# The expert stretch of a hybrid decoder layer on one core: larger weight transfers, and output sums that stay in PSUM

## The chip, the core and the metric

The kernel runs on one core of a Trainium2 chip. The core has TensorE (matmuls, from SBUF into the eight PSUM banks), VectorE and ScalarE (elementwise work), GpSimd (POOL) and SyncE (SP), whose instruction queue issues most of the DMA transfers here. The engines run side by side and wait for each other by semaphores. The metric is the device time of one execution in microseconds (us); less is better.

## The reference, cut to what matters

One layer over 16 learned and 256 given tokens of width 1024, all in float32. A mixing sub-layer comes first (sliding-window attention beside a state-space mixer, gated, summed, projected by `w_out`); the change leaves it alone but for a few loads. Then comes a top-4-of-32 expert network on the 256 tokens:

```
logits = u @ w_router + b_router;  top_w = softmax(top 4 of logits)
for each expert e, for the tokens tok routed to it with weights wt:
    hh = u[tok] @ w1[e] + b1[e]                 # 1024 -> 2048
    h  = min(hh[0::2],7) * sigmoid(1.702*min(hh[0::2],7)) * (clip(hh[1::2],-7,7) + 1)
    out[tok] += (h @ w2[e] + b2[e]) * wt        # 1024 -> 1024
out = rms_norm(residual + out) * g_final
```

The weights of one expert are 8 MiB (w1) and 4 MiB (w2); all 32 are read, 402.7 MB in all.

## The kernel before, in words

Everything before the expert stretch is a fixed program that ends with `w_out`, the norm and the router at about 560 us. In its last part TensorE multiplies by `w_out` for the first 128 tokens (c = 0) and then for the second (c = 1); between the chunks of c = 1 it transposes the normalised rows of c = 0 and computes their logits. VectorE adds the residual (L1036), scales the rows to `un` (L1043), and splits `un` into three bfloat16 parts `upart` (L1044 to L1048), which together hold the float32 value. Then it finds the four experts of each token and each token's place among its expert's rows (L1062 to L1087).

The expert stretch is a loop over 32 experts, the same in every engine's program, two experts per turn of TensorE's and SP's loops (even and odd). CAP = 64 rows are computed per expert; were an expert to get more tokens, further passes would run (`more`), which does not happen with these inputs. For expert t:

- VectorE makes one-hot matrices from the places (`gsel`, `gwt`, `bsel`; L1091 to L1094, function `routing`).
- TensorE gathers the tokens by 48 small bfloat16 matmuls with `gsel`, and starts the hidden sum in PSUM by the bias rows `b1all` (4 matmuls). VectorE copies the gathered rows, times the norm's gain, to `usel` (L1107).
- TensorE multiplies by w1 in eight parts of 1 MiB, first the four of hidden columns 0 to 1023 (half 0), then those of half 1. Each part is 4 matmuls of 512 columns with 64 stationary columns; two such matmuls fill the two halves of a PSUM bank's partitions.
- Between the halves it scatters the output of expert t-1: four matmuls of the weighted one-hot `s2` with `ysb`, each into bank 6 or 7, and VectorE adds each result to `acc` in SBUF (L1103), before the bank is used again. Then it transposes `gwt` (L1527), and ScalarE copies that to `s2` (L755).
- VectorE and ScalarE compute the clamped SwiGLU of each half (L1115 to L1119, L758). TensorE transposes the hidden rows (L1535), ScalarE copies them to `hT` (L761), and TensorE multiplies by w2 in four parts of 1 MiB. Half 1 is transposed after the w2 parts of half 0. The result lies in banks 2 and 3; ScalarE copies both to `ysb` (L765).

The weights arrive by SP's queue in parts of 128 partitions x 2 x 1024 numbers, so in runs of 4 KiB. Twelve of the parts go to the twelve slots of `ring`. Parts 0 to 3 have a second buffer for odd experts, in `arena` (`DOUBLED`), so 16 MiB can be under way or waiting. `step` sets the order of SP's queue: parts 0 to 3 of the next expert as this one's predecessor frees them, then parts 4 to 11 of this one; before each SP waits for `slot_used`, which TensorE raises after each part. `first_experts` and two places in the list of earlier chunks issue the first 16 parts as the mixing sub-layer frees the memory. After the loop come the last scatter, the sum of squares (L777), the reciprocal root on POOL (L494), the final scaling (L1160) and the store (L481).

All matmuls are issued by one helper, so they stand under L1169. A float32 matmul is two instructions in the profile.

## Time and profile before

| | us |
|---|---|
| median of 3 runs (1538.6 to 1541.98) | 1541.2 |
| the profiled execution: span from first to last instruction | 1541.4 |
| TensorE busy | 1397.1 (91%) |
| VectorE busy | 503.4 (33%) |
| ScalarE busy | 321.0 (21%) |
| first gather of the expert stretch begins | 559.8 |
| last w2 matmul ends | 1527.8 |

The profiled execution's own time is the span; it agrees with the median of the other runs to 0.2 us. The chip is asked for 470.77 MB in all, 305 GB/s over the span. The page divides the span into 40 slices of 38.5 us and shows for each the busy share of an engine in tenths, the granted TensorE clock in tenths of 2.4 GHz, and DMA. A busy engine need not be the one that decides; what decides in a stretch is read from who waits for whom there.

### The profile page before, as it was taken

The numbers are of one execution on the slowest core, as the hardware profiler recorded it, in microseconds if no ns is written. First come the engines' busy times: TensorE is split into PE (matmuls) and PEld (weight loads), VectorE is DVE, ScalarE is ACT, GpSimd is POOL, SyncE is SP. The second block draws the span as 40 slices with busy tenths as digits, with TensorE's granted clock in tenths as the row PEclk, the third lists the DMA queues.
The fourth block names the chain that finished last, engine by engine and source line by source line (L and its number), as shares of the span: only waits on it lengthen the run. The fifth ranks groups of instructions, "written<-read, shape, count | busy, mean of one in ns | idle before, by whom it ended". The sixth has DMA issues, their size and how long they took to land.

```text
span 1541.4 us, 19865 instructions
## 1 busy us (share of the span) xinstructions
PE 1397.1 (91%) x7262; PEld 679.1 (44%) x7262; DVE 503.4 (33%) x1075; ACT 321.0 (21%) x642; POOL 23.3 (2%) x33
## 2 busy tenths in 40 slices
PE   6359999999999969999999999999999999999997
PEld 3238878755588533333333333333333333333332
DVE  1004546657723253223223322322332232223223
ACT  3002433334410021211121121112112111211121
POOL 2010000000000000000000000000000000000000
PEclk9769999999999979999999999999999999999999
DMA  9996144314293579999999999999999999999993
GB/s 180 104 220 215 55 126 145 113 55 109 69 293 136 198 245 401 410 410 409 409 410 410 410 410 409 409 410 410 410 410 410 409 409 410 410 410 410 409 409 131
DMA packets 165814, 470.77 MB, mean 305 GB/s; under 512 B 24198, under 2 KB 59246, under 8 KB 165748
## 3 DMA queue, kind: packets, MB, share of 16 engines
q1 hardware_dynamic: 162544, 457.27, 78.3%
q0 software_dynamic: 2880, 12.63, 5.2%
q10 hardware_dynamic: 356, 0.41, 0.1%
q8 instruction: 21, 0.34, 0.1%
q14 instruction: 13, 0.11, 0.0%
HBM read 462.42 MB, written 7.60 MB: 305 GB/s over the span
## 4 chain that ended last, share of the span: by engine, by line
PE 72%; SPq 12%; DMA 8%; DVE 4%; ACT 2%; issue 1%; ACTq 0%; POOL 0%; POOLq 0%; DVEq 0%
PE bank L1169 70%; SPq L401 7%; DMA ring<-in_w 6%; SPq L414 5%; DVE arena L1107 1%; DMA ring<-in_w_in 1%; ACT arena L761 1%; DVE arena L1115 1%; ACT arena L758 1%; PE bank L1535 1%; DMA rows<-in_g_ssm 0%; PE bank L1527 0%; PE bank L1254 0%; PE bank L1429 0%; PE bank L1256 0%
## 5 line engine op out<-in xcount | busy, mean ns | idle before, releaser
L1169 PE MATMUL bank<-ring,arena 128*64 128x512 f32 (+3 forms) x2808 | 677.1, 594 | 53.9 <-ACT arena L761 45.6
L1169 PEld LDWEIGHTS bank<-ring,arena 128*64 128x64 f32 (+2 forms) x2808 | 219.2, 141 | 435.5 <-issue 365.6
L1169 PE MATMUL bank<-arena 128*128 128x64 bf16 (+6 forms) x2773 | 370.9, 337 | 13.8 <-DVE arena L1073 4.1
L1169 PE MATMUL bank<-arena,ring 128*128 128x256 f32 (+1 forms) x1184 | 276.4, 392 | 46.5 <-DMA ring<-in_w_in 43.9
L1169 PEld LDWEIGHTS bank<-arena 128*128 128x128 bf16 (+3 forms) x2773 | 173.4, 125 | 221.0 <-issue 145.9
L1169 PEld LDWEIGHTS bank<-arena,ring 128*128 128x128 f32 x1184 | 227.8, 195 | 85.3 <-issue 45.7
L1103 DVE TENSOR_TENSOR arena<-arena,bank 128x512 f32<-128x512 f32 x128 | 87.9, 687 | 292.4 <-PE bank L1169 292.4
L1107 DVE TENSOR_TENSOR arena<-bank,cols 128x512 f32<-128x512 f32 x32 | 22.1, 691 | 292.5 <-PE bank L1169 292.5
L755 ACT ACTIVATE arena<-bank 128x256 f32<-128x256 f32 x32 | 12.3, 383 | 360.1 <-PE bank L1527 360.1
L758 ACT ACTIVATE arena<-arena 128x256 f32<-128x256 f32 x64 | 26.6, 416 | 172.3 <-DVE arena L1115 172.3
L765 ACT ACTIVATE arena<-bank 128x512 f32<-128x512 f32 x64 | 34.7, 595 | 127.0 <-PE bank L1169 127.0
L1115 DVE TENSOR_SCALAR arena<-bank 128x256 f32<-128x256 f32 x64 | 27.1, 424 | 80.5 <-PE bank L1169 75.7
L761 ACT ACTIVATE arena<-bank 128x256 f32<-128x256 f32 x64 | 24.0, 374 | 132.9 <-PE bank L1535 132.9
L755 ACT ACT_TABLE_LOAD x32 | 41.1, 1283 | 0.6
L758 ACT ACT_TABLE_LOAD x32 | 41.1, 1283 | 0.6
L1535 PEld LDWEIGHTS bank<-squares,arena 128*128 128x128 f32 x128 | 12.9, 141 | 51.9 <-issue 51.9
L818 DVE TENSOR_TENSOR dts<-dts,dtb 128x96 f32<-128x96 f32 x1 | 0.3, 259 | 89.8 <-ACT dts L594 89.8
L1535 PE MATMUL bank<-squares,arena 128*128 128x128 f32 x128 | 28.0, 301 | 0.0
L1119 DVE TENSOR_TENSOR arena<-arena 128x256 f32<-128x256 f32 x64 | 27.2, 425 | 2.2
L1117 DVE SCALAR_TENSOR_TENSOR arena<-arena 128x256 f32<-128x256 f32 x64 | 27.2, 425 | 2.2
L1116 DVE TENSOR_SCALAR arena<-bank 128x256 f32<-128x256 f32 x64 | 27.1, 424 | 2.2
L494 POOL TENSOR_TENSOR rstd<-ssq,half_neg 128x1 f32<-128x1 f32 (+2 forms) x7 | 6.2, 888 | 1347.4 <-DVE ssq L1158 974.9
(221 smaller groups left out, 593.3 us busy)
## 6 DMA issues: line engine op xcount, KB each, us to landing
ring<-in_w SPq DMA_DIRECT2D x320, 1024.0 KB, 18.3
arena<-in_w SPq DMA_DIRECT2D x64, 1024.0 KB, 18.2
ring<-in_w_in SPq DMA_DIRECT2D x30, 1024.0 KB, 5.5
ring<-in_w_ssm SPq DMA_DIRECT2D x8, 1024.0 KB, 5.9
toep_rows<-arena POOLq DMA_DIRECT2D x1, 6400.0 KB, 68.6
ring<-in_w_in SPq DMA_DIRECT2D x16, 256.0 KB, 9.2
ring<-in_w_att SPq DMA_DIRECT2D x16, 256.0 KB, 6.5
ring<-in_w_out SPq DMA_DIRECT2D x4, 1024.0 KB, 4.8
```

The lines of the kernel that those rows point to most:

```text
L401: sp.dma_start(dst, src).then_inc(loaded, 16)
L414: sp.dma_start(dst(n % FSLOTS), src).then_inc(slot_loaded[n % FSLOTS], 16)
L755: sc.activation(s2, bank[5][:, 0:SEQ], ACT.Copy).then_inc(s2_saved, 1)
L758: sc.activation(sig[:, half, :], glu[:, half, :], ACT.Sigmoid, scale=ALPHA).then_inc(esig_ready, 1)
L761: sc.activation(hT[:, half, :, :], bank[5][:, 0:256].rearrange("p (b n) -> p b n", b=2), ACT.Copy).then_inc(hT_saved, 1)
L765: sc.activation(ysb[:, n, :], bank[2 + n][:, :], ACT.Copy).then_inc(ye_saved, 1)
L1103: done(v.tensor_tensor(a, a, bank[6 + n][:, :], ALU.add), sc_added, s * 4 + (i + 2))
L1107: done(v.tensor_tensor(usel, bank[4][:, :].rearrange("p (k s) -> p k s", k=KT), col_gffn.unsqueeze(2).to_broadcast([P, KT, CAP]), ALU.mult ...
L1115: done(v.tensor_scalar(glu[:, half, :], hv[:, :, 0], LIMIT, None, ALU.min), glu_ready, t * 2 + half + 1)
L1117: ch.link(v.scalar_tensor_tensor(lin[:, half, :], lin[:, half, :], 1.0, glu[:, half, :], ALU.add, ALU.mult))
L1169: return tn.matmul(o, lhsT, rhs, start=first, stop=last, skip_group_check=True)
L1535: ins = tn.transpose(bank[5][:, P * q:P * q + P], hsw[:, half, P * q:P * q + P], ident)
```

## The change

- w1's parts are rows 2p and 2p+1 of a block of 256 rows for partition p, all 2048 columns: 16 KiB in one run. A part is 2 MiB, and there are four. w2's two parts of 2 MiB hold two rows of 1024 next to each other, twice: runs of 8 KiB. The order of the contraction rows changes with it, so `un`, the norm's gain, the router's weights and the transposes of `hsw` take their elements with a stride.
- Six parts have a buffer for even experts, the four of w1 a second one for odd experts: ten buffers, 20 MiB. The first loads are spread anew over the waits of the earlier program.
- The output sum lies in banks 0 to 3 over all experts. It starts with the residual, put there by identity matmuls (`residual`), and the scatter adds to it in place. VectorE's additions go. w2's result is one bank: output columns 0 to 511 on partitions 0 to 63, the rest on partitions 64 to 127. The scatter's four matmuls contract over 64 rows each, the upper or the lower half.
- TensorE's order within an expert: bias rows, all of w1, the gather for expert t+1, the scatter of t-1, the transposes of the slot weights, all four transposes of hidden rows, w2. `usel` of t+1 is thus made during expert t.
- The final sum of squares and scaling read PSUM.

```diff
+        even_bufs = [at(6400, BUF), ring_pair(4), at(R, BUF), at(R + 6144, BUF), ring_pair(1), ring_pair(5)]
+        odd_bufs = [ring_pair(0), ring_pair(2), ring_pair(3), at(0, BUF)]
+        DOUBLED = range(len(odd_bufs))
...
+        w1_v = w1.rearrange("e (s p k) c -> e s p (k c)", p=P, k=2)
+        w2_v = w2.rearrange("e (h c p q) n -> e h p c (q n)", p=P, c=2, q=2)
...
+            src = [w1_v[ahead:][one, s].rearrange("e p f -> p (e f)") for s in range(4)]
+            src += [w2_v[ahead:][one, h].rearrange("e p c f -> p (e c) f") for h in range(2)]
...
+                    for i in range(2):
                         fetch(i, sources[0][i], 0)
-                    fetch(DOUBLED[2], sources[1][DOUBLED[2]], 1)
+                if n == co[0]:
+                    sp.wait_ge(tile_ready, T_END)
+                    fetch(2, sources[0][2], 0)
...
             def first_experts():
...
+                sp.wait_ge(branch_used, 12)
+                fetch(3, sources[0][3], 0)
+                fetch(4, sources[0][4], 0)
+                sp.wait_ge(m_done, 8)
+                fetch(5, sources[0][5], 0)
+                sp.wait_ge(h_ready, 2)
+                for i in range(3):
                     fetch(i, sources[1][i], 1)
-                for i in range(SLOTS):
-                    if slot_of(i) in late:
-                        sp.wait_ge(h_ready, 2)
-                        fetch(i, sources[0][i], 0)
-                sp.wait_ge(topexp_in, 1)
-                fetch(DOUBLED[3], sources[1][DOUBLED[3]], 1)
+                sp.wait_ge(lg_ready, 1)
+                fetch(3, sources[1][3], 1)
...
+                    pool.wait_ge(up_done, 1)
...
-                    pool.dma_start(gfin, bass.AP(g_fin.tensor, 0, [[0, P], [1, D]])).then_inc(gfin_in, 16)
+                    pool.wait_ge(b2_cleared, 1)
+                    for half in range(2):
+                        pool.dma_start(ysb[CAP * half:CAP * half + E, :], b2[:, 512 * half:512 * half + 512]).then_inc(b2_in, 16)
...
+            def s2_save(n):
+                act.wait_ge(s2_ready, n + 1)
+                sc.activation(s2, bank[6][:, 0:SEQ], ACT.Copy).then_inc(s2_saved, 1)
...
+                s2_save(t + 1)
...
-                act.wait_ge(slot_used, t * 12 + 12)
-                for n in range(2):
-                    sc.activation(ysb[:, n, :], bank[2 + n][:, :], ACT.Copy).then_inc(ye_saved, 1)
+                act.wait_ge(slot_used, t * PARTS + PARTS)
+                sc.activation(ysb, bank[6][:, :], ACT.Copy).then_inc(ye_saved, 1)
...
-            for c in range(2):
-                act.wait_ge(acc_final, 2 * c + 2)
-                squared(sc.activation(at(0, D), acc[:, c, :], ACT.Square,
-                                      accum_out=ssq[:, c:c + 1]), 13 + c + 1)
+            for i in range(4):
+                act.wait_ge(last_sc_ready, i + 1)
+                squared(sc.activation(glu.rearrange("p a b -> p (a b)"), bank[i][:, :], ACT.Square,
+                                      accum_out=ssq[:, i:i + 1]), 13 + i + 1)
...
+                dve.wait_ge(resid_done, c + 1)
                 ch.link(v.tensor_tensor(ures[:, c, :], un[:, c, :], upart[:, 0, c, :], ALU.subtract))
...
-                ch.link(v.tensor_copy(upart[:, 2, c, :], ures[:, c, :]))
+                done(v.tensor_copy(upart[:, 2, c, :], ures[:, c, :]), up_done, c + 1)
...
+            def slots_of(col):
                 for c in range(2):
...
-            def scatter_add(s):
-                for i in range(4):
-                    c, n = divmod(i, 2)
-                    dve.wait_ge(sc_ready, s * 4 + (i + 1))
-                    a = acc[:, c, 512 * n:512 * n + 512]
-                    done(v.tensor_tensor(a, a, bank[6 + n][:, :], ALU.add), sc_added, s * 4 + (i + 2))
+                    ins = v.tensor_scalar(gsel[:, c, :], iota2[:, 0:CAP], pos[:, c, bass.ds(col, 1)], None, ALU.is_equal)
+                ins.then_inc(g_ready, 1)
...
+            def slot_weights(col, n):
+                dve.wait_ge(s2_ready, n)
+                for c in range(2):
+                    ins = v.tensor_scalar(gwt[:, c, :], iota2, pos[:, c, bass.ds(col, 1)], wtok[:, c, bass.ds(col, 1)],
+                                          ALU.is_equal, ALU.mult)
+                ins.then_inc(gw_ready, 1)
+            def usel_save(n):
+                dve.wait_ge(gat_ready, n + 1)
+                v.tensor_tensor(usel, bank[7][:, :].rearrange("p (k s) -> p k s", k=KT),
+                                col_gffn.unsqueeze(2).to_broadcast([P, KT, CAP]), ALU.mult).then_inc(usel_ready, 1)
...
+                    if half == 0:
+                        dve.wait_ge(hid_ready, t + 1)
+                    else:
+                        dve.wait_ge(slot_used, t * PARTS + 4)
+                    hv = bank[4 + half][:, :].rearrange("p (f two) -> p f two", two=2)
...
+                usel_save(t + b + 1)
+                slots_of(e + 2)
+                bias_row(e + 1)
+                slot_weights(e + 1, t + 2)
...
-            for i in range(4):
-                c, n = divmod(i, 2)
-                dve.wait_ge(last_sc_ready, i + 1)
-                a = acc[:, c, 512 * n:512 * n + 512]
-                done(v.tensor_tensor(a, a, bank[6 + n][:, :], ALU.add), acc_final, i + 1)
...
+                for n in range(2):
+                    ins = v.scalar_tensor_tensor(fin[:, c, 512 * n:512 * n + 512], bank[2 * c + n][:, :], rstd[:, 4 + c:5 + c],
+                                                 gfin[:, 512 * n:512 * n + 512], ALU.mult, ALU.mult)
...
+            def residual(c):
+                pe.wait_ge(h_done, 2 * c + 2)
+                for n in range(2):
+                    ins = mm(bank[2 * c + n][:, :], ident, acc[:, c, 512 * n:512 * n + 512], True, True)
+                ins.then_inc(resid_done, 1)
...
+                        residual(0)
...
+            residual(1)
...
-            def scatter(s):
-                for i in range(4):
-                    c, n = divmod(i, 2)
-                    if i < 2:
-                        pe.wait_ge(sc_added, s * 4 + 1)
-                    else:
-                        pe.wait_ge(sc_added, s * 4 + i)
-                    mm(bank[6 + n][:, :], s2[:, P * c:P * c + P], ysb[:, n, :], True, True).then_inc(sc_ready, 1)
...
+            def gather(n):
+                pe.wait_ge(g_ready, n + 1)
...
+            def scatter(n):
+                pe.wait_ge(ye_saved, n + 1)
+                pe.wait_ge(s2_saved, n + 1)
+                for c in range(2):
+                    for half in range(2):
+                        r = slice(CAP * half, CAP * half + CAP)
+                        ins = mm(bank[2 * c + half][:, :], s2[r, P * c:P * c + P], ysb[r, :], False, True)
...
+                pe.wait_ge(usel_ready, t + b + 1)
+                for i in range(4):
...
-                    if half == 0:
-                        pe.wait_ge(ye_saved, t * 2 + 2)
-                        scatter(t)
-                        for c in range(2):
-                            ins = tn.transpose(bank[5][:, P * c:P * c + P], gwt[:, c, :], ident)
-                        ins.then_inc(s2_ready, 1)
-                pe.wait_ge(s2_saved, t + 1)
+                                c0 = 1024 * half + 512 * c
+                                ins = mm(bank[4 + half][64 * c:64 * c + 64, :], usel[:, k, :], w[:, kk, c0:c0 + 512],
+                                         False, k == KT - 1)
+                        if i == 3 and half == 0:
+                            ins.then_inc(hid_ready, 1)
...
+                gather_wait = t * 1 + b * 2 + 1
+                gather(gather_wait)
+                scatter(t)
+                weight_transposes(t + b + 1)
                 for half in range(2):
                     pe.wait_ge(hs_ready, t * 2 + half + 1)
-                    if half:
-                        pe.wait_ge(hT_saved, t * 2 + 1)
                     for q in range(2):
-                        ins = tn.transpose(bank[5][:, P * q:P * q + P], hsw[:, half, P * q:P * q + P], ident)
+                        ins = tn.transpose(bank[4 + half][:, P * q:P * q + P], hsw[:, half, q::2], ident)
                     ins.then_inc(hT_ready, 1)
+                pe.wait_ge(s2_saved, t + 2)
+                for half in range(2):
...
+                    expert_arrived(pe, 4 + half, t, pair, odd)
+                    w = expert_buf(4 + half, odd)[0].rearrange("p (c q n) -> p c q n", c=2, q=2)
...
+                            for n in range(2):
+                                ins = mm(bank[6][64 * n:64 * n + 64, :], hT[:, half, q, 64 * c:64 * c + 64],
+                                         w[:, c, q, 512 * n:512 * n + 512],
+                                         half == 0 and c == 0 and q == 0, half == 1 and c == 1 and q == 1)
...
+            gather(0)
+            weight_transposes(0)
+            pe.wait_ge(b2_in, 32)
             pe.wait_ge(b1_spread, 32)
+            pe.wait_ge(flag_ready, 1)
```

What stands on three queues before and now. First TensorE, from the last w1 part of half 0 of an odd expert to the start of w2. Before (`sc_added` is raised by VectorE's additions, `more_loaded` and `slot_loaded` by weight transfers):

```order
L1169 MATMUL bank<-arena 64x512 [waits more_loaded3]
L1169 MATMUL bank<-arena 64x512 x3
L1524 ISA
L1492 ISA [waits ye_saved]
L1169 MATMUL bank<-arena 128x512 [waits sc_added] x2
L1494 REGISTER_ALU
L1169 MATMUL bank<-arena 128x512 [waits sc_added]
L1494 REGISTER_ALU
L1169 MATMUL bank<-arena 128x512 [waits sc_added]
L1527 MATMUL bank<-squares,arena 128x128 x2
L374 ISA
L1169 MATMUL bank<-ring,arena 64x512 [waits slot_loaded11]
```

And now, from the last w1 part of an odd expert on:

```order
L1194 MATMUL bank<-arena 64x512 [waits odd_loaded3]
L1194 MATMUL bank<-arena 64x512 x7
L1522 REGISTER_ALU
L1194 MATMUL bank<-arena 128x64 [waits g_ready]
L1194 MATMUL bank<-arena 128x64 x47
L1194 MATMUL bank<-arena 128x512 [waits s2_saved,ye_saved]
L1194 MATMUL bank<-arena 128x512 x3
L1534 MATMUL bank<-squares,arena 128x128 [waits gw_ready]
L1534 MATMUL bank<-squares,arena 128x128
L1572 ISA
L1574 MATMUL bank<-squares,arena 128x128 [waits hs_ready]
L1574 MATMUL bank<-squares,arena 128x128
```

The gather and the scatter have moved between w1 and the transposes of the hidden rows, and the waits for VectorE's additions between the scatter's matmuls are gone.

Second TensorE at the end of `w_out`, before the first expert. Before, the last `w_out` chunk follows the router's matmuls, and the transposes of c = 1 follow that:

```order
L1169 MATMUL bank<-wrt,arena 128x32 [waits u2_saved]
L1169 MATMUL bank<-wrt,arena 128x32 x3
L1169 MATMUL bank<-ring,arena 128x512 [waits slot_loaded0]
L1169 MATMUL bank<-ring,arena 128x512 x3
L1444 MATMUL bank<-squares,arena 128x128 [waits un_ready]
L1444 MATMUL bank<-squares,arena 128x128 x7
```

Now:

```order
L1194 MATMUL bank<-wrt,arena 128x32 [waits u2_saved]
L1194 MATMUL bank<-wrt,arena 128x32 x3
L1194 MATMUL bank<-arena,squares 128x512 [waits h_done]
L1194 MATMUL bank<-arena,squares 128x512
L1194 MATMUL bank<-ring,arena 128x512 [waits slot_loaded0]
L1194 MATMUL bank<-ring,arena 128x512 x3
L1194 MATMUL bank<-arena,squares 128x512 [waits h_done]
L1194 MATMUL bank<-arena,squares 128x512
L1472 MATMUL bank<-squares,arena 128x128 [waits un_ready]
```

Two pairs of identity matmuls have come in, one ahead of the last chunk and one behind it.

SP's queue keeps the order of its parts, w1 of the next expert and then the rest of this one; the transfers per expert fall from twelve to six. The last two experts are issued as before: the single parts of expert 30, then all of expert 31.

## Rows read from the trace of the kernel before

**Rows 1.** The page's 40 slices: DMA share in tenths, rate.
```profile
DMA  9996144314293579999999999999999999999993
GB/s 180 104 220 215 55 126 145 113 55 109 69 293 136 198 245 401 410 410 409 409 410 410 410 410 409 409 410 410 410 410 410 409 409 410 410 410 410 409 409 131
```

**Rows 2.** DMA issues to the ring: number, size, median us to landing.
```profile
ring<-in_w SPq DMA_DIRECT2D x320, 1024.0 KB, 18.3
```

**Rows 3.** Timeline, VectorE's usel operation: start, duration, idle before.
```profile
1254.29 0.69 DVE L1107 TENSOR_TENSOR arena<-bank,cols 128x512 f32<-128x512 f32 x1 [9.84 <-PE bank L1169]
1285.01 0.69 DVE L1107 TENSOR_TENSOR arena<-bank,cols 128x512 f32<-128x512 f32 x1 [9.92 <-PE bank L1169]
```

**Rows 4.** Weight queue's waits for DMA, 600 to 1200 and 1225 to 1500.
```profile
PEld bank L1169 <- DMA ring<-in_w: 0.3, 1, 0.3
...
PEld bank L1169 <- DMA ring<-in_w: 27.3, 32, 1.2
```

**Rows 5.** Timeline of TensorE over one expert.
```profile
995.20 7.09 PE L1169 MATMUL bank<-ring,arena 128*64 128x512 f32 x32
1002.22 0.44 PE L1535 MATMUL bank<-squares,arena 128*128 128x128 f32 x2
1003.53 3.65 PE L1169 MATMUL bank<-ring,arena 128*64 128x512 f32 x16 [0.88 <-ACT arena L761]
1007.12 0.44 PE L1535 MATMUL bank<-squares,arena 128*128 128x128 f32 x2
1008.11 3.65 PE L1169 MATMUL bank<-ring,arena 128*64 128x512 f32 x16 [0.55 <-ACT arena L761]
1011.69 2.13 PE L1169 MATMUL bank<-arena 128*128 128x64 bf16 x52
1014.05 10.98 PE L1169 MATMUL bank<-arena 128*64 128x512 f32 x40 [0.23 <-DVE arena L1107]
1024.86 0.38 PE L1527 MATMUL bank<-squares,arena 128*128 128x128 f32 x2
1025.17 7.09 PE L1169 MATMUL bank<-ring,arena 128*64 128x512 f32 x32
```

**Rows 6.** Windows: stretch, length, five engines, granted clock, DMA share, GB/s.
```profile
380.00:390.00 10.00, 10.00 (x38) 5.48 (x37) 6.54 (x11) 3.41 (x6) 0.00 (x0) 1.00 0.26 83
464.00:467.00 3.00, 3.00 (x15) 2.66 (x14) 0.00 (x0) 0.00 (x0) 0.00 (x0) 1.00 0.95 331
516.00:530.00 14.00, 14.00 (x34) 6.25 (x33) 3.00 (x6) 1.15 (x2) 0.83 (x2) 1.00 1.00 352
1400.00:1500.00 100.00, 93.24 (x562) 32.99 (x558) 25.31 (x55) 19.06 (x31) 0.00 (x0) 1.00 1.03 410
1510.00:1515.00 5.00, 5.00 (x23) 1.91 (x24) 3.51 (x9) 1.99 (x3) 0.00 (x0) 1.00 0.50 202
```

**Rows 7.** Timeline of SP's queue: late first loads, the first freed part.
```profile
541.15 2.23 SPq L401 DMA_DIRECT2D ring<-in_w  x4
...
566.04 26.07 SPq L401 DMA_DIRECT2D ring<-in_w  x12
```

**Rows 8.** Timeline ahead of the first expert, VectorE and TensorE.
```profile
531.97 1.23 DVE L1047 TENSOR_TENSOR arena<-arena 128x1024 f32<-128x1024 f32 x1
533.23 0.69 DVE L1048 CAST arena<-arena 128x1024 bf16<-128x1024 f32 x1
...
537.44 3.68 PE L1169 MATMUL bank<-ring,arena 128*128 128x512 f32 x8
541.23 1.42 DVE L1036 TENSOR_TENSOR arena<-bank,arena 128x512 f32<-128x512 f32 x2 [7.31 <-PE bank L1169]
563.28 7.69 PE L1169 MATMUL bank<-ring,arena 128*64 128x512 f32 x32
```

**Rows 9.** Timeline of the last w2 matmuls and the store.
```profile
1524.16 3.65 PE L1169 MATMUL bank<-ring,arena 128*64 128x512 f32 x16 [0.55 <-ACT arena L761]
1529.16 3.93 PE L1169 MATMUL bank<-arena 128*128 128x512 f32 x8 [1.35 <-ACT arena L765]
```

More of the change, by code:

```diff
@@ L55 @@
 FSLOTS = 7
+PARTS = 6
+BUF = 2 * SLOT
 NEG = -1e30
@@ new lines, in hybrid_layer @@
+        ysb = at(4224, 512)
+        rt = at(4736, 16, 64)
+        glu, sig = at(4736, 2, 256), at(5248, 2, 256)
+        s2 = at(5760, SEQ)
+        gwt = at(6016, 2, P)
+        usel = at(R + 4096, KT, CAP)
+        hT = at(R + 4608, 2, 2, P)
+        lin = hsw = at(R + 5120, 2, 256)
+        SM = R + 13312
+        gsel = at(SM, 2, CAP, dt=BF16)
+        bsel = at(SM + 64, CAP, dt=BF16)
+        pos = at(SM + 96, 2, 40)
+        wtok = at(SM + 176, 2, 40)
+        ident3 = at(SM + 256, 40)
@@ L399, in fetch @@
             def fetch(i, src, odd):
-                dst, loaded = expert_slot(i, odd)
+                dst, loaded = expert_buf(i, odd)
+                if i >= 4:
+                    dst = dst.rearrange("p (c f) -> p c f", c=2)
                 sp.dma_start(dst, src).then_inc(loaded, 16)
@@ L442, in single @@
             def single(sources, odd, used):
-                for i in range(DOUBLED.stop, SLOTS):
+                for i in range(DOUBLED.stop, PARTS):
                     sp.wait_ge(slot_used, used + (i + 1))
@@ L1174, in _ @@
             tn.transpose(bank[4][:, 0:120], rows[0:120, 0, :], ident[0:120, 0:120])
-            tn.transpose(bank[4][:, 128:160], rows[0:32, 1, :], ident[0:32, 0:32]).then_inc(rows_T, 1)
+            tn.transpose(bank[4][:, 128:152], rows[0:24, 1, :], ident[0:24, 0:24])
+            for k in range(2):
+                ins = tn.transpose(bank[4][:, 160 + 4 * k:164 + 4 * k], gffn4[0:4, k::2], ident[0:4, 0:4])
+            ins.then_inc(rows_T, 1)
             pe.wait_ge(tab_ready, 1)
@@ L1508, in expert @@
                         c0 = 1024 * half + 512 * c
-                        mm(bank[half][64 * c:64 * c + 64, :], bsel[0:3 * E, :], b1all[0:3 * E, c0:c0 + 512], True, False)
-                pe.wait_ge(usel_ready, t + 1)
-                for half in range(2):
-                    for s_ in range(4):
-                        i = 4 * half + s_
-                        expert_arrived(pe, i, t, pair, odd)
-                        w, _ = expert_slot(i, odd)
+                        mm(bank[4 + half][64 * c:64 * c + 64, :], bsel[0:3 * E, :], b1all[0:3 * E, c0:c0 + 512], True, False)
@@ L1555, in _ @@
                 with pe.Fori(0, PASSES - 1) as b:
+                    gather(b * G_PASS + G_PASS)
                     with pe.Fori(0, E // 2) as pair:
```

273 lines of the change are left out of this document (117 added, 156 removed).

## The prediction

> **What bounds the kernel now.** I read the page's slices first [rows 1]: from slice 17 to 39 the DMA row stands at 9 and the GB/s row at 409 to 410. TensorE is busy there too, 93.24 of 100 us in the window from 1400 us [rows 6]. So for some 900 of 1541.4 us two resources are full at once, and the busy shares can't say which one sets the pace. The DMA issues [rows 2] say what the traffic is: transfers of 1 MiB, twelve per expert, of which ten go to the ring. Each lands 18 us after its issue, so seven are under way at a time and DMA never lacks work. Next the distance between experts: on TensorE 29.97 us from the second half of w1 to the next [rows 5], later, by VectorE's one usel operation per expert, 30.72 (1254.29 to 1285.01 [rows 3]). The weight queue's waits separate the two [rows 4]: between 600 and 1200 us TensorE waited for a weight transfer once (0.3 us), between 1225 and 1500 us 32 times (27.3 us). 12 MiB (12.58 MB) in 30.72 us is 409.6 GB/s, exactly the saturated rate. So the first 20-odd experts run at TensorE's own period of 30.0 us, eating up what had been loaded ahead, and the last nine or so at the transfers' 30.7. A change of this stretch has to shorten both, or it gives at most 0.7 us on a third of the experts.
>
> TensorE's 29.97 us of one expert [rows 5], start to start: first half of w1 with the scatter 10.81 (1014.05 to 1024.86), of which the half itself is 7.02 (995.20 to 1002.22, the other half alone), so the scatter 3.79; transposes of the slot weights 0.31 (to 1025.17); second half of w1 7.02; transposes of the hidden rows and the wait for ScalarE's copy 1.31; w2 3.59; the same wait again 0.99; w2 3.58; gather, bias rows and the wait for usel 2.36.
>
> **What the change does to TensorE's period.** The weight matmuls stay: 32 and 16 of them, 14.04 and 7.17 us. Gather and bias rows stay, 2.13 us (52 instructions), but their 0.23 us wait for usel goes, since gather n+1 now runs behind w1 of expert n and usel is ready 10 us early. Slot-weight transposes 0.31. The hidden rows' four transposes are issued together, so one of the two waits for ScalarE remains: 1.31 instead of 1.31 + 0.99. VectorE has time: half 0 is released four matmuls (1.8 us) before w1 ends, its chain of four 0.42 us operations and that of half 1 end 2.1 us behind w1, and TensorE is then still in gather and scatter (1.6 + 1.7 us). The scatter has four matmuls of 512 columns as before, without the VectorE additions between them. The trace does not show a matmul with 64 contraction rows beside another one, so I bound it: at the dearest it costs what the row of eight instructions says without waits, some 3.5 us; at the cheapest the two 64-row halves run side by side, as the two 64-column halves of the weight matmuls do (two of them every 0.88 us, 7.02 / 8, against 0.87 to 0.95 for one full-width matmul), 1.75 us. I take the cheap end, the likeness to the column halves being close; both are kept.
> Period: 14.04 + 7.17 + 2.13 + 0.31 + 1.31 + 1.75 = 26.7 us; with the dear scatter 28.5.
> The Trainium skill (TensorEngine Tiling (Array Packing), section Tiling Modes) lists two 64x128 tiles that run in parallel, which gives the 1.75 us, but adds that a change of tiling mode drains the engine; by that the scatter could be some tenths dearer, and no row here shows a drain's price.
>
> **What it does to the transfers.** Four w1 transfers with 16 KiB runs and two w2 transfers with 8 KiB runs take the place of twelve with 4 KiB runs; the bytes are the same. The windows [rows 6] give the price of a run from share and rate. 4 KiB runs: 410 GB/s at share 1.03, so 4096 x 16 x 1.03 / 410 = 164.6 ns a packet. 1 KiB runs (the w_ssm chunks): 1024 x 16 x 0.95 / 331 = 47.0 ns in one window, 51.3 in another (0.26, 83). A straight line through them rises by (164.6 - 47.0) / 3 = 39.2 ns per KiB and leaves 7.8 ns per packet, or by (164.6 - 51.3) / 3 = 37.8 and leaves 13.5. Carried on to 16 KiB that is 635 or 618 ns, so 16384 x 16 x 1.03 / 635 = 425 GB/s, or 437; to 8 KiB 321 or 316 ns, so 420 or 428. I take values nearer to the low line, whose window has the fuller DMA: 428 and 422. The ends of the unknown, since no queue of SP shows runs over 4 KiB: no gain (410), above 437, and below the worst 4 KiB stretch, 352 GB/s at share 1.00.
> The Trainium skill (DMA: Bandwidth & Descriptors, section Where 436 GB/s comes from) puts the ports' ceiling at 435 GB/s. By that my upper line is cut by 2 GB/s, and the gain can't pass 6%; the trace, at 410, is under the ceiling.
>
> A transfer period is then 8.39 MB / 428 + 4.19 MB / 422 = 19.60 + 9.94 = 29.5 us, above TensorE's 26.7 and 28.5. So the transfers become the bound early, and stay it.
>
> **Before the first expert.** Before, the last of the 16 MiB of first loads were four parts when h was ready, at 541.15, and one behind the logits; then none until the first part was used, at 566.0 [rows 7]. Now 4 MiB go out when y is done, as before, 2 ahead of w_out (SP waits there for the last transposes of the branch stage, behind which w_out's loads are queued; they are done by then), 6 at the end of the branch products, 6 when h is ready and 2 at the logits: 20 MiB. What is added to the path there: the residual sum enters PSUM by two 512-column identity matmuls ahead of the last w_out chunk, at 0.92 us each (3.68 / 4 [rows 8]), +1.8 us on everything behind. VectorE's splitting of u for the first 128 tokens now waits for that, until about 539.3 (537.44 + 1.8), and takes 4.0 us with its gaps (1.23 + 0.69 twice), to 543.3; behind it stands the h addition that began at 541.23. So +2.1 in all, not +1.8. The second pair of identity matmuls lies in the time in which TensorE waits for the norm of c = 1. The normalised rows are written with a stride; for that I put 0.4. Against that, the gather of expert 0 waits for two selection operations rather than five: three fewer, -1.1. Behind VectorE's wait for the residual nothing else queues but those operations, and POOL's queue (the clearing of ysb, two b2 transfers, then the next rstd) is through at about 545, before the sum of squares is, which begins with that h addition's end. w1 of expert 0 starts at 563.28 + 2.1 + 0.4 - 1.1 = 564.7, and its first 2 MiB are free after half of 7.69 us: 568.5.
>
> **The sum.** In the run before, 16 of 384 MiB were issued before 566.0; the other 368 MiB are 385.9 MB, 941.2 us at 410; the stream ended at 1512.5 (window 1510 to 1515: share 0.50), 946.5 us after 566.0, so 5.3 us went with getting up to speed. I keep these. After: 364 MiB remain at 568.5. SP issues w2 of expert 30 before w1 of expert 31, and from the landing of expert 29's w2 on, 16 MiB are left (39 us of transfers) but two whole experts of TensorE (53 us), so TensorE bounds the end. Until that landing: 232 MiB of w1, 243.3 MB / 428 = 568.4 us, and 116 MiB of w2, 121.6 MB / 422 = 288.2. Landing at 568.5 + 5.3 + 568.4 + 288.2 = 1430.4. Then the last half of w2 3.6 and two experts, 53.4: 1487.4. The cross-check by TensorE alone, 564.7 + 32 x 26.7 = 1419 (1477 with 28.5), lies below, so the transfers decide. The end: before, 13.6 us from w2's last matmul (1527.8) to 1541.4 [rows 9]. One PSUM copy less -0.5, the scatter 3.93 to about 2.0 and no VectorE additions -2.2; four half-size squares on ScalarE with their sums instead of two +0.9: 11.8. Total 1487.4 + 11.8 = 1499 us. The profiled span of before is 1541.4, the median of the runs 1541.2, so nothing is to be converted. 2.7% faster. Where it comes from: transfers' rate some 34 us, deeper preloading and the shorter period of TensorE the rest.
>
> **The rivals.**
> A. Longer runs are no faster: the fixed part lies per 4 KiB, not per run. For it: no SP transfer here has a longer run. Against: packets of 1 and 4 KiB lie on a line with a fixed part. 364.9 MB / 410 = 890.0, landing at 1463.8, + 57.0 + 11.8 = 1532.6. Chance 0.14.
> B. TensorE stays the bound: scatter unpaired and a wait of 1.5 us more (for s2 or the hidden rows, which no longer have a w1 half between them): period 30, 564.7 + 960 + 11.8 = 1536.5. Against: every releaser has slack of 1 us or more in the working above. Unpaired alone costs only 2 x 1.8 at the end: 1503. Chance 0.04.
> C. Slower than before: the long runs lower the rate, as they would if reading rows 16 KiB apart in step, or filling one partition for 0.6 us on end, cost the memories something. Decisive is 406 GB/s: (1541.4 - 11.8 - 57.0 - 5.3 - 568.5) = 898.8 us for 364.9 MB. At 400 GB/s the landing is at 1486.1 and the time 1555; at the 352 of [rows 6] it is 1679. For it: the 352 itself, 4 KiB runs that did not reach 410 when they began with other traffic. Against: 900 us at 410 with w1's rows 8 KiB apart. Chance 0.07.
> [...]
> D. The upper line, 437 and 428: 556.7 + 284.2 us, so 1483.5. It is part of the forecast's own range.
>
> **How the numbers follow.** Forecast case 0.73, from 1484 to 1512; A 0.14, B 0.04, C 0.07, and 0.02 for a step I don't see. Range: from 1484 up to A's and B's place with their uncertainty, 1536; outside lie C and the remains. What a measurement can tell from no change is 0.2%, 3 us: under 1538.1 lie the forecast, A in most of its spread and half of B: 0.87; within 0.2%: 0.05; above: 0.08.
>
> **What would show it.** A GB/s row of about 425 in slices 16 to 37 and larger transfers; distances between usel operations of 26 to 27 us for the first experts (28.5: scatter unpaired) and 29.5 later; TensorE's waits for DMA at the w2 parts, some 2.8 us per expert; the scatter's eight instructions in under 2 us; usel of expert 0 some 1.4 us later; the end in 12 us. Wrong it would be with 410 in that row (A), less (C), or waits on ScalarE or VectorE in the place of DMA (B).

## The result, and the profile after

| kernel | median of the runs | range | profiled span |
|---|---|---|---|
| before | 1541.59 us | 1538.6 to 1542.06 | 1541.4 us |
| changed | 1497.48 us | 1495.86 to 1497.97 | 1496.1 us |

The ratio is 0.9715, with a 95% interval of 0.9703 to 0.9728: 44.1 us or 2.85% faster. Forecast were 1499 us, within 1484 to 1536.

The page's slices of the changed kernel, which answer to [rows 1]: DMA share in tenths, then the rate.

```profile
DMA  9997134322367458999999999999999999999994
GB/s 183 104 203 251 58 107 140 119 85 57 113 232 239 173 226 365 427 427 425 426 428 427 423 427 428 427 424 427 427 426 425 429 427 424 427 428 427 424 379 177
```

The DMA row is as full as it was, so a share of 9 says nothing of whether more would go through. The rate says it: 427 where it was 410. The page's list of DMA issues (number, size, median us from issue to landing) shows what makes the stream now; before, it was one row of 1 MiB transfers [rows 2].

```profile
ring<-in_w SPq DMA_DIRECT2D x128, 2048.0 KB, 25.6
arena<-in_w SPq DMA_DIRECT2D x64, 2048.0 KB, 29.5
```

The chain that ended last, shares of the span by engine. Before, it held 72% TensorE and 8% DMA; now DMA holds 43%.

```profile
PE 47%; DMA 43%; SPq 5%; DVE 2%; ACT 1%; issue 1%; ACTq 0%; POOL 0%; DVEq 0%; POOLq 0%
```

An early expert on the timeline of TensorE, which answers to [rows 5] (start, duration, group; in brackets the idle time before it and what ended it):

```profile
661.54 7.09 PE L1194 MATMUL bank<-ring,arena 128*64 128x512 f32 x32 [0.46 <-ACT arena L764]
668.45 4.04 PE L1194 MATMUL bank<-arena 96*64 96x512 bf16 x20
672.32 3.61 PE L1194 MATMUL bank<-ring,arena 128*64 128x512 f32 x16
675.75 10.47 PE L1194 MATMUL bank<-arena 128*64 128x512 f32 x88
686.15 0.44 PE L1534 MATMUL bank<-squares,arena 128*128 128x128 f32 x2
686.42 0.64 PE L1574 MATMUL bank<-squares,arena 128*128 128x128 f32 x4
687.52 7.22 PE L1194 MATMUL bank<-ring,arena 128*64 128x512 f32 x32 [0.46 <-ACT arena L764]
```

From one w2 to the next it is 25.98 us (687.52 less 661.54), w2 itself 6.91 in one piece, and the only wait left is 0.46 us for ScalarE. The same engine at a late expert:

```profile
1273.54 0.64 PE L1574 MATMUL bank<-squares,arena 128*128 128x128 f32 x4
1276.46 3.65 PE L1194 MATMUL bank<-ring,arena 128*64 128x512 f32 x16 [2.29 <-DMA ring<-in_w]
1281.53 3.65 PE L1194 MATMUL bank<-ring,arena 128*64 128x512 f32 x16 [1.41 <-DMA ring<-in_w]
...
1302.98 0.64 PE L1574 MATMUL bank<-squares,arena 128*128 128x128 f32 x4
1305.98 3.65 PE L1194 MATMUL bank<-ring,arena 128*64 128x512 f32 x16 [2.36 <-DMA ring<-in_w]
```

In these two experts TensorE stands still twice, 3.7 us in all, each time ahead of a half of w2, and the distance is 29.52 (1305.98 less 1276.46). 12.58 MB in 29.5 us is 427 GB/s: the transfers set the pace. By VectorE's usel operation the 2nd to the 6th distance are 25.98 to 26.12, the 7th to the 31st 29.4 to 29.6, and the last is 25.98.

The end, TensorE's last three groups, and the end of expert 29's w2 ahead of them:

```profile
1424.03 8.78 PE L1194 MATMUL bank<-ring,arena 128*64 128x512 f32 x32 [2.36 <-DMA ring<-in_w]
1432.64 4.04 PE L1194 MATMUL bank<-arena 96*64 96x512 bf16 x20
...
1477.69 7.09 PE L1194 MATMUL bank<-ring,arena 128*64 128x512 f32 x32 [0.46 <-ACT arena L764]
1485.47 1.99 PE L1194 MATMUL bank<-arena 64*128 64x512 f32 x8 [0.69 <-ACT arena L767]
```

The scatter's eight instructions take 1.99 us, where [rows 9] had 3.93.

Expert 29's w2 has no second wait, but takes 8.78 us in one piece: the granted clock is at its lower level (1.2 GHz) from 1424.8 to 1428.2, right behind the wait of 2.36 us. A window inside that stretch (five engines, granted clock, DMA share, GB/s; the stream runs empty in it, because SP holds w2 of expert 30 back until expert 29's is used):

```profile
1426.00:1428.00 2.00, 2.00 (x8) 0.64 (x6) 0.00 (x0) 0.00 (x0) 0.00 (x0) 0.50 0.44 184
```

By the trace, 25 experts in a row, up to this one, have such a wait of 2.3 to 2.4 us ahead of w2. 10 of them have the second wait of 1.4 us as well; in the other 15 the clock falls during or just behind the first wait, and the second wait is missing. That costs nothing that shows, since the second part of w2 lands only then (at 1428.9 for expert 29). gather2, below, has no such fall of the clock and the same late distance of 29.5 us.

### The profile page after: what moved, and what is told of

Read it like the earlier page. It is cut to its first block, busy times and chain, and to the rows that moved or that the text cites. A ratio compares the mean times of both kernels' runs of the same rounds, so it can differ in the third digit from the quotient of the medians.

```text
span 1496.1 us, 18512 instructions
## 1 busy us (share of the span) xinstructions
PE 1333.6 (89%) x7320; PEld 697.8 (47%) x7320; DVE 397.9 (27%) x952; ACT 261.8 (18%) x584; POOL 22.4 (1%) x32
## 4 chain that ended last, share of the span: by engine, by line
PE 47%; DMA 43%; SPq 5%; DVE 2%; ACT 1%; issue 1%; ACTq 0%; POOL 0%; DVEq 0%; POOLq 0%
PE bank L1194 45%; DMA ring<-in_w 41%; SPq L421 5%; DMA ring<-in_w_in 1%; DMA rows<-in_g_ssm 0%; PE bank L1282 0%; PE bank L1457 0%; PE bank L1284 0%; PE bank L1534 0%; ACT arena L755 0%; DVE arena L1055 0%; DVE arena L1053 0%; PE bank L1348 0%; ACT arena L611 0%; DVE ring L908 0%
## 5 line engine op out<-in xcount | busy, mean ns | idle before, releaser
L1194 PE MATMUL bank<-ring,arena 128*64 128x512 f32 (+3 forms) x2296 | 579.0, 613 | 76.9 <-DMA ring<-in_w 72.6
L1194 PE MATMUL bank<-arena 128*128 128x64 bf16 (+7 forms) x3333 | 418.3, 372 | 11.6 <-DVE arena L1081 5.2
L1194 PEld LDWEIGHTS bank<-ring,arena 128*64 128x64 f32 (+2 forms) x2296 | 204.8, 147 | 411.2 <-issue 341.2
L1194 PEld LDWEIGHTS bank<-arena 128*128 128x128 bf16 (+4 forms) x3333 | 204.7, 126 | 226.8 <-issue 205.3
L760 ACT ACTIVATE arena<-arena 128x256 f32<-128x256 f32 x64 | 26.7, 417 | 394.4 <-DVE arena L1126 394.4
L767 ACT ACTIVATE arena<-bank 128x512 f32<-128x512 f32 x32 | 19.1, 597 | 315.6 <-PE bank L1194 315.6
L1109 DVE TENSOR_SCALAR arena<-squares,arena 128x128 f32<-128x128 f32 x66 | 19.9, 344 | 36.0 <-PE bank L1534 36.0
L755 ACT ACTIVATE arena<-bank 128x256 f32<-128x256 f32 x32 | 12.3, 383 | 93.2 <-PE bank L1534 93.2
L908 DVE SCALAR_TENSOR_TENSOR ring<-ring,cols 128x272 f32<-128x272 f32 x48 | 24.1, 502 | 1.7
L1033 DVE TENSOR_TENSOR arena<-ring,bank 128x512 f32<-128x512 f32 x8 | 5.5, 687 | 62.6 <-PE bank L1194 62.4
L764 ACT ACTIVATE arena<-bank 128x256 f32<-128x256 f32 x64 | 21.0, 385 | 0.0
L1194 PE MATMUL bank<-arena,squares 128*128 128x512 f32 x40 | 19.0, 597 | 2.1 <-DVE arena L1041 2.1
## 6 DMA issues: line engine op xcount, KB each, us to landing
arena<-in_w SPq DMA_DIRECT2D x64, 2048.0 KB, 29.5
```

What stands on the lines that cost most here:

```text
L760: sc.activation(sig[:, half, :], glu[:, half, :], ACT.Sigmoid, scale=ALPHA).then_inc(esig_ready, 1)
L764: sc.activation(hT[:, half, :, :], bank[4 + half][:, 0:256].rearrange("p (b n) -> p b n", b=2), ACT.Copy).then_inc(hT_saved, 1)
L767: sc.activation(ysb, bank[6][:, :], ACT.Copy).then_inc(ye_saved, 1)
L908: ch.link(v.scalar_tensor_tensor(o, xp[:, k:k + NT], w(k), o, ALU.mult, ALU.add))
L1109: ins = v.tensor_scalar(gwt[:, c, :], iota2, pos[:, c, bass.ds(col, 1)], wtok[:, c, bass.ds(col, 1)], ALU.is_equal, ALU.mult)
L1194: return tn.matmul(o, lhsT, rhs, start=first, stop=last, skip_group_check=True)
```

## The experiments

Every kernel below is the changed one with one edit, timed beside the kernel before on the same chip (1540.6 to 1541.2 us there; differences to the changed kernel's 1497.48 are thus good to about 1 us). In the diffs "-" is the changed kernel.

**runs4k: the changed kernel with the runs of before.** It asks whether run length is what pays.

```diff
-        w1_v = w1.rearrange("e (s p k) c -> e s p (k c)", p=P, k=2)
+        w1_v = w1.rearrange("e (s p k) (h c) -> e s p h k c", p=P, k=2, h=2)
-        w2_v = w2.rearrange("e (h c p q) n -> e h p c (q n)", p=P, c=2, q=2)
+        w2_v = w2.rearrange("e (h c p q) n -> e h p q c n", p=P, c=2, q=2)
...
-                sp.dma_start(dst, src).then_inc(loaded, 16)
+                for h in range(2):
+                    sp.dma_start(dst[:, h], src[h]).then_inc(loaded, 16)
```

> The changed kernel (1497.5 us) with each 2 MiB part loaded as two transfers of 1 MiB in runs of 4 KiB, as before; buffers, TensorE's order and PSUM sums stay as changed. Theory 1 (the run length sets the transfers' rate, and that rate sets the pace from the seventh expert on): GB/s row at 410 again, usel operations 30.7 us apart later, 26.0 at the start; some 33 us more, 1531. Theory 2 (TensorE's shorter period brought the gain, the runs little): within 5 us of 1497. If 1531 comes, the rest of the change is worth 10 us against the kernel before.

Measured: 1533.64 us (1533.24 to 1537.0), ratio to before 0.9957 [0.9943, 0.9971]. Its slices, and TensorE at a late expert:

```profile
GB/s 181 104 218 222 56 125 141 120 55 110 80 284 192 172 277 407 409 409 409 410 410 409 410 410 410 410 409 410 410 410 409 410 410 410 409 409 410 410 333 208
```

```profile
1275.19 8.87 PE L1194 MATMUL bank<-ring,arena 128*64 128x512 f32 x32 [3.42 <-DMA ring<-in_w]
...
1305.91 6.29 PE L1194 MATMUL bank<-ring,arena 128*64 128x512 f32 x20 [3.42 <-DMA ring<-in_w]
```

The rate is back at 410 and the distance at 30.72 us, with everything else of the change in place. So 36.2 of the 44.1 us are run length (1533.64 less 1497.48), and the shorter period of TensorE, the deeper stock and the shorter end together give 7 to 8. That is less than the 10 that I expected; where the rest went is open.

**runs8k: all runs 8 KiB, in 1 MiB transfers.** It parts the length of a run from the size of a transfer.

```diff
-        w1_v = w1.rearrange("e (s p k) c -> e s p (k c)", p=P, k=2)
+        w1_v = w1.rearrange("e (s p k) c -> e s p k c", p=P, k=2)
...
-                sp.dma_start(dst, src).then_inc(loaded, 16)
+                for k in range(2):
+                    sp.dma_start(dst[:, SLOT * k:SLOT * k + SLOT], src[k]).then_inc(loaded, 16)
```

> The changed kernel with each part as two transfers of 1 MiB, but all in runs of 8 KiB. Theory 1 (a fixed cost per run of 8 to 9 ns): rate 421 GB/s, periods 29.9, 1506 to 1507. If the size of a transfer (1 MiB for 2 MiB) counted and not the run, it would be as slow as with runs of 4 KiB, 1531, at 410.

Measured: 1505.05 us (1503.84 to 1507.26), 0.9771 [0.9755, 0.9787]. The window from 900 to 1000 us (five engines, granted clock, DMA share, GB/s):

```profile
900.00:1000.00 100.00, 90.67 (x540) 35.85 (x538) 14.82 (x42) 12.83 (x23) 0.00 (x0) 0.97 1.01 422
```

At 1 MiB the transfers carry 422 GB/s with 8 KiB runs and 410 with 4 KiB runs, so the gain comes without larger transfers. The reverse shows too: each run is one packet in the trace's DMA records, and an 8 KiB packet takes 314 ns on average between 900 and 1000 us, in the 1 MiB transfers here and in the 2 MiB transfers of the changed kernel alike. The run decides, not the transfer's size. The 7.6 us to the changed kernel are w1's runs, 8 KiB for 16: a late distance of 29.84 for 29.52 us.

**stock16: 4 MiB less loaded ahead.**

```diff
-                for i in range(3):
+                for i in range(2):
                     fetch(i, sources[1][i], 1)
-                sp.wait_ge(lg_ready, 1)
+                sp.wait_ge(slot_used, 1)
+                fetch(2, sources[1][2], 1)
```

> The changed kernel, but the last two of the ten first loads wait for the first freed part, so 16 MiB are loaded before the experts begin instead of 20. Theory 1: each MiB not loaded ahead comes at the end at 2.45 us, so 9.8 us more: 1507; the transfers become the bound four experts earlier. Rival (depth is without effect, the queue is full anyhow): 1497.5.

Measured: 1506.51 us (1505.03 to 1507.94), 0.9773 [0.9757, 0.9789]: 9.0 us slower than the changed kernel, where 4.19 MB at 427 GB/s are 9.8. The usel distances after the first read 25.97, 25.98, 28.32 and then 29.5. Where the transfers set the pace, what is loaded before the stretch is worth about its transfer time.

**gather2 and gather4: TensorE given more to do.** The gather's matmuls are issued twice or four times, with the same result.

```diff
-                for k in range(KT):
+                for k in [k for _ in range(4) for k in range(KT)]:
```

> The changed kernel with the 48 gather matmuls of each expert issued four times: some 4.7 us more of TensorE per expert, period 30.6 instead of 26.0. Theory 1: above the transfers' 29.5, so TensorE is the bound and only the part over it counts: 564.7 + 32 x 30.6 + 12 = 1556 to 1561, GB/s row at about 411, with the long runs unused. A theory in which TensorE's time counts in full: 1497.5 + 32 x 4.7 = 1648; one in which it doesn't count: 1497.5.

Measured for gather4: 1548.23 us (1545.72 to 1548.39), 1.0047 [1.0031, 1.0064]. The distance is 30.19 us at a late expert:

```profile
1253.77 7.09 PE L1194 MATMUL bank<-ring,arena 128*64 128x512 f32 x32 [0.46 <-ACT arena L764]
...
1283.95 7.09 PE L1194 MATMUL bank<-ring,arena 128*64 128x512 f32 x32 [0.46 <-ACT arena L764]
```

The waits for transfers are gone. A repeat costs 1.40 us, (30.19 - 25.98) / 3, less than the 1.57 that I had put (4.7 / 3), so the time came out 8 us below the range that was expected.

> The gather matmuls are issued twice, same result, one repeat costing TensorE 1.40 us per expert by the kernel with them fourfold. Theory (the transfers set the pace up to expert 29's w2, TensorE has 29.5 - 26.0 = 3.5 us of slack): distances of 27.4 at first, 29.5 later, and only the first expert's gather and the two experts behind the last landing count: 1497.5 + 1.4 + 2 x 1.4 = 1501.7, range 1499 to 1503. Rival (TensorE sets the pace for part of each period, through the waits at w2): + 32 x 1.4 = 1542; a mixture 1510 to 1520.

Measured for gather2: 1501.52 us (1500.86 to 1502.03), 0.9745 [0.9729, 0.9761], against 1501.7 forecast. The distances were 27.38 us at first and 29.5 from the tenth on. Of 32 x 1.4 = 45 us that TensorE has more to do, 4.0 show, against the 4.2 expected for the first expert's repeat and the last two experts'. The rest lies in the 3.5 us in which TensorE waits anyway.

**scatter_order and scatter_one: do the two 64-row halves run side by side?** The first only reorders the four matmuls, both of one half and then both of the other. The second sends all four to rows 0 to 63; it leaves the second half's outputs out and counts the first's twice.

```diff
 scatter_order
-                for c in range(2):
-                    for half in range(2):
+                for half in range(2):
+                    for c in range(2):
 scatter_one
-                        r = slice(CAP * half, CAP * half + CAP)
+                        r = slice(0, CAP)
```

> The changed kernel with the scatter's four matmuls in another order, both of rows 0 to 63 first, then both of rows 64 to 127. If it is the two different row halves that run side by side, only the middle two can now: the eight instructions inside an expert take some 2.6 us instead of 1.8. If each matmul is simply cheap with 64 rows, the time stays. Device time in either case within 3 us of 1497.5, since TensorE waits for transfers.

Measured, one run: 1496.81 us, and the early distances stay 25.98 to 26.00. The 2.6 us did not come. By the expectation as I had written it, this would speak for matmuls that are cheap with 64 rows, and against the halves running side by side; the next run says otherwise.

> All four scatter matmuls of an expert read rows 0 to 63 (half 0), in the loop and behind it, so the second half's outputs are left out and the first's counted twice; number and size of the matmuls stay. Theory (the two halves run side by side on the array, which is where 3.93 us became 1.99): in one half they can't, so the scatter behind the last expert takes 3.5 to 4.0 us, the distance between usel operations of the first experts is 25.98 + 1.7 = 27.7, and the time is 1497.5 + 2 x 1.7 + 0.2 = 1501. Rival (a matmul that reads 64 rows costs half of one that reads 128, alone or beside another): 1.99 us, 25.98 and 1497, as changed.

Measured, one run: 1503.08 us. The distances are 27.69, and the scatter behind the last expert:

```profile
1490.48 3.70 PE L1194 MATMUL bank<-arena 64*128 64x512 f32 x8 [0.69 <-ACT arena L767]
```

3.70 against 1.99 us, and 27.69 less 25.98 is 1.71 us, the saving forecast for the pair. So a 64-row matmul alone costs nearly what a 128-row one does (3.93 for four in [rows 9]), and it is the sharing of the array that halves it. The instruction records of an early expert show how. In the changed kernel the eight instructions start in four pairs, 7 ns apart within a pair; in scatter_one they start one by one, 0.43 to 0.54 us apart. In scatter_order they start in four pairs too, 13 ns apart, though both matmuls of the first half stand in the queue ahead of both of the second. Since two of one half don't start together, each pair must be one of each half. So the second half's work starts beside the first half's and doesn't wait for what is queued ahead of it on the other half, which is where my 2.6 us went wrong.

**endswap and allswap: w2 ahead of the next w1 in SP's queue.** In the changed kernel TensorE waits at w2 while 8 MiB of the next w1, which it needs later, go ahead of it in the queue. endswap turns the order round in the last three turns of SP's loop, allswap in every turn.

```diff
-                doubled(following, 1 - odd, used)
-                single(sources, odd, used)
+                if swap:
+                    single(sources, odd, used)
+                doubled(following, 1 - odd, used)
+                if not swap:
+                    single(sources, odd, used)
```

> The changed kernel, but for the turns of experts 27, 28 and 29 SP issues w2 of the expert ahead of w1 of the next one. Theory 1: in the transfer-bound stretch TensorE always waits for a w2 part that stands in the queue behind four w1 parts it needs later; at the end this leaves two experts (52 us) of TensorE with only 39 us of transfers beside them. With three turns swapped the last three to five experts run at 26 us: 9 to 10 us less, 1488. Rival: the queue's order doesn't matter, the same bytes are to come: 1497.5.

Measured: 1489.26 us (1487.99 to 1490.82), 0.9665 [0.9652, 0.9679]: 8.2 us faster than the changed kernel. Its last waits for transfers are these, at the third and the last of the four parts of the last w1:

```profile
1448.59 7.11 PE L1199 MATMUL bank<-ring,arena 128*64 128x512 f32 x32
1457.34 3.65 PE L1199 MATMUL bank<-ring,arena 128*64 128x512 f32 x16 [1.65 <-DMA ring<-in_w]
1462.24 7.08 PE L1199 MATMUL bank<-arena 128*64 128x512 f32 x72 [1.24 <-DMA arena<-in_w]
```

Three distances ahead of them are 25.98, where the changed kernel had one, its last. In the changed kernel 39 us of transfers follow the last one that TensorE waits for; endswap uses a part of that.

> The changed kernel with w2 of the expert ahead of w1 of the next one in every turn. Theory 1: SP's wait for the previous expert's w2 to be used then holds up w1 transfers whose buffers are long free, so that DMA stands idle in the first experts, where TensorE sets the pace, and the ten buffers are not refilled; that costs more than the end gains: some 1506, GB/s under 420 in slices 16 to 19. If only the end's balance counted: 1488.

Measured: 1503.93 us (1502.92 to 1504.52), 0.976 [0.9744, 0.9775]: 6.4 us slower than the changed kernel. Its slices tell why:

```profile
GB/s 183 104 206 245 57 112 141 114 82 73 95 259 224 199 227 156 427 426 425 428 427 425 427 428 426 424 427 427 426 424 428 427 424 427 428 427 424 427 427 248
```

The 16th slice, with the first expert in it, has 156 GB/s where the changed kernel has 365. SP's first turn now waits for w2's buffers of expert 0 (used last), and the freed w1 buffers behind that wait stay empty. From 552 to 586 us SP issues nothing, where the changed kernel's first freed part goes out at 568.8. (365 - 156) GB/s over a slice of 37.5 us is 7.8 MB, 18 us of stream in that slice; in all, the last weights land 13.6 us later than endswap's (1485.7 for 1472.2 us by the traces). The end itself is as good as endswap's, 16.9 us from that landing to the end of the span in both, but it doesn't make this good.

**both: endswap, and w2 in 16 KiB runs too.** The price of the longer runs is sixteen 64-column matmuls against the identity, where four transposes stood.

```diff
-        w2_v = w2.rearrange("e (h c p q) n -> e h p c (q n)", p=P, c=2, q=2)
+        w2_v = w2.rearrange("e (h p q) n -> e h p (q n)", p=P, h=2)
-                    for q in range(2):
-                        ins = tn.transpose(bank[4 + half][:, P * q:P * q + P], hsw[:, half, q::2], ident)
+                    for q in range(4):
+                        for c in range(2):
+                            r = slice(CAP * c, CAP * c + CAP)
+                            ins = mm(bank[4 + half][r, CAP * q:CAP * q + CAP], hsw[:, half, q::4], ident[:, r], True, True)
```

> As endswap, and w2's parts laid out so that a partition holds four successive rows: runs of 16 KiB for w2 too. The hidden rows are then transposed by sixteen matmuls with identity columns (128 x 64 x 64) instead of four transposes, at most 1 us more for TensorE, which is hidden while the transfers set the pace. Theory 1: period 29.4 instead of 29.5 and 428 GB/s throughout, 4 us under endswap less up to 3 us at the end: 1484 to 1487.

Measured: 1486.4 us (1484.23 to 1488.16), 0.9646 [0.9633, 0.966], the fastest kernel of this study, 11.1 us below the changed one. A window of it, and TensorE's timeline at the end:

```profile
900.00:1000.00 100.00, 93.91 (x629) 42.13 (x626) 15.82 (x45) 12.30 (x23) 0.00 (x0) 1.00 1.01 429
```

```profile
1437.37 2.13 PE L1197 MATMUL bank<-squares,arena 128*64 128x64 f32 x32
1439.34 7.04 PE L1197 MATMUL bank<-ring,arena 128*64 128x512 f32 x32
...
1466.24 7.04 PE L1197 MATMUL bank<-ring,arena 128*64 128x512 f32 x32
```

The rate is 429 and the late distance 29.36 us. TensorE's own period rises to 26.90 (1466.24 less 1439.34), where that is hidden. It is 2.9 us below endswap by the medians, but the two ranges touch (1487.99 to 1490.82 against 1484.23 to 1488.16), so that last step is likely rather than shown.

## Why the prediction was right, point by point

- **The bound.** Two resources were full before, and both had to become shorter. runs4k shows it from one side (TensorE at 25.98, transfers as before: 7 to 8 us), gather4 from the other (transfers as changed, TensorE slowed by added work to 30.19: 1548.23 us, 7 slower than before). Neither half of the change is worth much without the other.
- **The rate.** From rows of 1 and 4 KiB straight lines were carried on, and 422 and 428 GB/s chosen between them. Measured: 422 with 8 KiB runs alone, 429 with 16 KiB alone, 427 mixed. That there is a fixed part per run was right. That the choice met 427 so closely is luck in part: 428 at the share of 1.03 puts a 16 KiB run at 631 ns (16384 x 16 x 1.03 / 428), and it took 615 in the DMA records, at a share of 1.01. The steeper line, to which I leaned, was the wrong one (635 ns; the other gave 618), and the share that I kept at 1.03 was too high; the two nearly cancel. Rival A (the fixed part lies per 4 KiB) would have kept 410; it was priced at 1532.6 us, and runs4k, which makes 410 true, took 1533.64. Some 34 us were put to the rate, runs4k says 36.2.
- **Rival C.** No loss shows from rows 16 KiB apart or from filling a partition on end: no full slice is below 423. By the Trainium skill (DMA: Bandwidth & Descriptors, section Latency and other measured facts) copies were slower when the rows of neighbouring partitions lay 512 KiB or a larger power of two apart. In the weight loads here they lie 8 and 16 KiB apart, so no run bears this out or refutes it.
- **TensorE's period: mis-sized, 25.98 for 26.7.** w2 took 6.91 instead of 7.17 us: it runs in one piece, where I had added two of 3.59 and 3.58. Bias rows, w1, gather and scatter took 17.70 (668.45 to 686.15) instead of 14.04 + 2.13 + 1.75 = 17.92, and the transposes with their wait 1.37 (to 687.52) instead of 0.31 + 1.31. For the matmuls, durations of pieces that ended at a wait or a change of operation were a little too long for work in one piece. At the transposes the wait for ScalarE itself is shorter, 0.46 us where [rows 5] had 0.88.
- **The paired scatter.** Taking the cheap end was right: by scatter_one pairing saves 1.71 us, and 1.75 was the difference between my two ends. The term itself was a little small. From the scatter's first instruction to the first transpose behind it are 1.92 us in the instruction records, where I had put 1.75; bias rows and gather (1.94 for 2.13) and w1 (13.84 for 14.04) hid that in the sum. The Trainium skill (TensorEngine Tiling (Array Packing), section Tiling Modes) says that a change of tiling mode drains the engine. The 0.17 us would fit that, at the low end of the tenths that I had named: 0.53 us pass from the first pair to the second and from the last to the transposes, 0.43 between the others. But no run here separates a drain from other costs of beginning and ending a group.
- **Before the first expert.** The h addition began at 543.50, 2.3 us later than in [rows 8] (2.1 forecast), and the first freed part was reissued at 568.77 (568.5 forecast). That it agrees to 0.2 us is luck in part: in three kernels that are the same up to there (scatter_order, endswap, allswap) the addition begins at 542.62, 543.54 and 542.03. The two rows of the changed kernel:

```profile
543.50 1.42 DVE L1041 TENSOR_TENSOR arena<-bank,arena 128x512 f32<-128x512 f32 x2
```

```profile
568.77 0.36 SPq L406 DMA_DIRECT2D arena<-in_w  x1
```

- **The landing and the end.** Expert 29's last w2 part landed at 1428.9 (1430.4 forecast). Thence 55.9 us to the end of the last w2 at 1484.8 (57.0 forecast, with two periods of 0.7 us more), and 11.3 us to the end of the span (11.8 forecast). The sum forecast was 1499.2 for a span of 1496.1: 1.5 of the 3.1 us come from the landing, 1.1 from the last two experts, 0.5 from the end.
- **Rival B** needed a period of 30: every wait that it feared was absent but 0.46 us for ScalarE.
- **What the prediction didn't see:** that "TensorE bounds the end" was a loss one could take back. 16 MiB land unwaited-for behind the last transfer that counts; turning two groups of transfers round in three turns of the queue is worth 8 us.

## What to carry to other kernels

When two resources are full at once, price a change on each side alone: the runs with one side undone stood 8 us below the kernel before and 7 us above it, the whole change 44 below. This stream, with DMA full in both kernels, still gained 4% from longer contiguous runs, so compare GB/s, not DMA share, and read the price per packet from two run lengths that the trace has. Then look at the last awaited transfer and at what is queued ahead of it; the right order at the end of a stream need not be the right one at its start, where a wait at the queue's head leaves freed buffers empty.

## What the runs showed of the hardware

- One core's stream from memory ran at 410, 422 and 429 GB/s with runs of 4, 8 and 16 KiB. At DMA shares of 1.03, 1.01 and 1.01 that is 165, 314 and 617 ns per run on each of 16 engines (4096 x 16 x 1.03 / 410, and so on). The DMA records themselves give means of 163.7, 313.7 and 614.7 ns between 900 and 1000 us (runs4k, runs8k, both): 37.5 to 37.6 ns per KiB and a fixed 13 to 14 ns. In transfers of 1 and 2 MiB an 8 KiB run took the same 314 ns.
- Two 64-row matmuls of 512 columns on different halves of the rows share the array: 1.99 us for four, 3.70 if all use one half. Their order in the queue, alternating or both of one half first, made no difference (25.98 us early distance in both, one run of the latter).
- At 15 of the changed kernel's 25 waits of 2.3 to 2.4 us ahead of w2, TensorE's granted clock fell to 1.2 GHz during the wait or just behind it, and the w2 of expert 29 took 8.78 instead of 7.09 us. While the transfers set the pace, that cost nothing that shows.
